# First mixer of a transformer stack: recurrence products cut to 32 keys by 16 queries, inverse products cut to the blocks that the masks keep

## The chip, the cores and the metric

The kernel runs on one core of a Trainium2 chip. The metric is the device time of one execution in microseconds (us), median of several runs. Engines are named as in the profile: PE is TensorE's matmul side, PEld its weight loads, DVE is VectorE, ACT is ScalarE, POOL is GpSimd, SP the queue that issues the weight transfers.

## What is computed

Four layers in a row on 256 tokens of width 2048, all in fp32: a first mixer with two recurrences and an FFN, a second mixer with sparse attention and an FFN, then two small attention layers. The change lies in the first mixer alone. After one large projection it computes, per head (8 of each kind, width 128), over chunks of tokens:

```python
def _hgrn2(q, f_logit, i, lb):            # gated linear recurrence
    ...
    decay = jnp.exp(jnp.where(tril, b[:, :, :, None, :] - b[:, :, None, :, :], -jnp.inf))
    intra = jnp.einsum('bhtd,bhsd,bhtsd->bhts', qn, kn, decay)

def _gated_delta(q, k, v, beta, log_decay):   # delta rule
    ...
    L = jnp.where(tril & ~eye, jnp.einsum('bhncd,bhnsd->bhncs', kb, kc) * decay, 0.0)
    sol = lax.linalg.triangular_solve(L + eye, rhs, left_side=True, lower=True, unit_diagonal=True)
```

## The kernel before, in words

**The main stream.** All large products are `activations x weights`, split in a high and a low part, so that each is three matmuls: 128 tokens stationary, 512 weight columns moving (lines 1124 to 1126 for the projections, 1171 to 1173 for the output matrices). The weights come in slots of 512 KB: SP loads a slot into one of four RAW buffers, ACT writes its high part (line 1669), DVE subtracts to get the low part (line 2197), PE does the slot's 12 matmuls.

**The order.** `write_order` lists by hand every step of the kernel, in one list that each engine walks, doing what it has in each step. Between two slots of the main stream it puts the steps of the mixer: `gdn()` puts the delta rule's, `hgrn(hf)` the gated recurrence's. So on every engine the mixer's work is interleaved with the slots, in a fixed order; an engine that waits in a step holds back all that stands behind it. `gdn()` leaves at least one slot between a product and the next one that needs it.

**The gated recurrence** (`hg_l`, levels l = 0 to 6, for each half hf of the heads: 4 heads, 2 chunks i of 128 tokens). Level l joins blocks of m = 2^l tokens in pairs: the queries of the late block of a pair with the keys of the early one. PE multiplies (line 1391) all 128 keys of a chunk with its 64 late queries, for 4 heads and 2 chunks, 8 products; DVE scales keys and queries for the next level (lines 2522, 2523), multiplies up the spans (`longer`, line 2499) and takes from the product only what the level's mask keeps (`copy_predicated`, line 2534). Level 5 is already cut to 32 keys by 32 queries, two products where the others have one (line 1389), level 6 to 64 keys by 64 queries.

**The delta rule** needs the inverse of a unit lower triangular matrix of 128 x 128 per head, for each (hf, i). Its diagonal blocks of 16 are made on DVE (`gd_w`, `gd_e`). Then for l = 4, 5, 6 two diagonal blocks of m = 2^l are joined: `gd_y` multiplies LT with the inverse so far (line 1271, 4 heads, 128 x 128 each), DVE masks the result into Y (line 2439); `gd_x` multiplies again (line 1289, for l = 6 line 1287) and DVE subtracts the whole product from XX (line 2446); for l = 4 a transpose on DVE follows (line 2449), for l = 6 PE transposes before it (line 1276). Four units (hf, i) make 12 steps of each kind.

Of the kernel before, what the change touches and what calls it, by code (L numbers as in the profile page):

```python
# [10 lines left out]
ALU = mybir.AluOpType  # L11
# [165 lines left out]
def rep(ap, n):  # L177
    return ap.unsqueeze(1).to_broadcast([ap.shape[0], n, ap.shape[1]])


def v3(ap, a):
    return ap.rearrange("p (a b) -> p a b", a=a)
# [601 lines left out]
def build(nc, A, out):  # L784
    with ExitStack() as ctx:
# [9 lines left out]
        def steps(name, line=None, by=1):  # L795
            all_steps.append(Steps(ctx.enter_context(nc.semaphore(name)), line or Line(), by))
            return all_steps[-1]
# [25 lines left out]
        banks = Banks([PS[:, i, :] for i in range(8)])  # L823
# [9 lines left out]
        def w3(o, n, a):  # L833
            return v3(WORK[:, o:o + n], a)
# [24 lines left out]
        MKT, BAND, BLOCK, EYE = WORK[:, 8704:9088], WORK[:, 9088:9216], WORK[:, 9216:9344], WORK[:, 9344:9360]  # L859
# [4 lines left out]
        KBT, QT, LT, QK = (w3(2048 + 512 * j, 512, 4) for j in range(4))  # L864
        XX = WORK[:, 4096:5120].rearrange("p (h x n) -> p h x n", h=4, x=2)
        Y, LTM, S, U = KT, QT, w3(5120, 512, 4), KB
        RV, RW, KD, WT, QE = ADEC, DEC, DEC, KBT, KT

        def gd_cols(hf, i):
# [7 lines left out]
        HX, HK, HQ, HA = (WORK[:, a:a + 1024] for a in (5632, 6656, 7680, 9472))  # L877
# [3 lines left out]
        def of_chunk(x, i):  # L881
            return v3(x, 4)[:, :, 128 * i:128 * i + 128]

        def sides(x, m):
            x = x.rearrange("p (b s m) -> p b s m", s=2, m=m)
            return x[:, :, 0], x[:, :, 1]
# [129 lines left out]
        def slot_of(s):  # L1016
# [3 lines left out]
            if wd < 64:  # L1020
# [10 lines left out]
        v_lo, v_ut, v_ff, v_nm, v_gd, v_cv, v_hg, v_og, v_ns, v_b2, v_rs = (  # L1031
            steps("s_dve_" + n, dve) for n in ("weights", "operand", "ffn", "norm", "gdn", "conv", "hgrn",
                                               "gate", "nsa", "block2", "root"))
# [31 lines left out]
        def tensor(e):  # L1065
# [7 lines left out]
            def take(*name):  # L1073
                b = banks.take(ring, *name)
                on.wait_ge(*banks.free(*name))
                return b
# [189 lines left out]
            @step  # L1266
            def gd_y(hf, i, l):
                b = take("y", hf, i, l)
                on.wait_ge(*(v_gd.of("x", hf, i, l - 1) if l > 4 else v_gd.of("xT", hf, i, 4)))
                for h in range(4):  # L1270
                    x = e.matmul(b[:, 128 * h:128 * h + 128], LT[:, h], XX[:, h, 0], start=True, stop=True)
                x.then_inc(*p_gd.inc("y", hf, i, l))
                if l == 6:
                    b = take("xT", hf, i, l)
                    for h in range(4):
                        x = e.transpose(b[:, 128 * h:128 * h + 128], XX[:, h, 0], ident)
                    x.then_inc(*p_gd.inc("xT", hf, i, l))

            @step
            def gd_x(hf, i, l):  # L1280
                b = take("x", hf, i, l)
                on.wait_ge(*v_gd.of("y", hf, i, l))
                on.wait_ge(*(a_gd if l == 6 else v_gd).of("xT", hf, i, l))
                for h in range(4):
                    o = b[:, 128 * h:128 * h + 128]
                    if l == 6:
                        x = e.matmul(o, Y[:, h], XX[:, h, 1], start=True, stop=True)
                    else:
                        x = e.matmul(o, XX[:, h, 1], Y[:, h], start=True, stop=True)
                x.then_inc(*p_gd.inc("x", hf, i, l))  # L1290

            @step
# [83 lines left out]

            @step
            def hg_l(hf, l):
                rows = 64 if l == 6 else 128
                b = take("hl", hf, l)  # L1380
                on.wait_ge(*v_hg.of("up", hf, l))
                for h in range(4):
                    for i in range(2):
                        late = sides(of_chunk(HQ, i)[:, h], 2 ** l)[1]
                        o = b[0:rows, 128 * h + 64 * i:128 * h + 64 * i + 64].rearrange("p (b m) -> p b m", m=2 ** l)
                        if l == 5:
                            for u in range(2):
                                k = slice(64 * u, 64 * u + 32)
                                x = e.matmul(o[k, u], of_chunk(HK, i)[:, h, k], late[:, u], start=True, stop=True)
                            continue  # L1390
                        x = e.matmul(o, of_chunk(HK, i)[:, h, 0:rows], late, start=True, stop=True)  # L1391
                x.then_inc(*p_hg.inc("s", hf, l))

            @step
# [791 lines left out]
        def vector(e):  # L2186
# [248 lines left out]

            @step
            def gd_y(hf, i, l):
                on.wait_ge(*p_gd.of("y", hf, i, l))
                e.tensor_tensor(Y, v3(banks.ap("y", hf, i, l), 4), rep(MKT[:, 128 * l - 512:128 * l - 384], 4),
                                ALU.mult).then_inc(*banks.empty(v_gd, "y", hf, i, l))  # L2440

            @step
            def gd_x(hf, i, l):
                o = XX[:, :, int(l == 6)]
                on.wait_ge(*p_gd.of("x", hf, i, l))
                e.tensor_tensor(o, o, v3(banks.ap("x", hf, i, l), 4), ALU.subtract).then_inc(*banks.empty(v_gd, "x", hf, i, l))
                if l < 5:
                    on.wait_ge(*v_gd.last())
                    e.transpose(XX[:, :, 1], XX[:, :, 0]).then_inc(*v_gd.inc("xT", hf, i, l + 1))
# [570 lines left out]
```

## Time and profile before

| | |
|---|---|
| median of 3 runs | 2727.71 us (2725.29 to 2728.68) |
| the profiled execution's own time | 2729.03 us |
| its span, first to last instruction | 2727.2 us |
| granted TensorE clock, mean | 0.997 of full |
| busy: PE / PEld / DVE / ACT / POOL | 2694.4 / 2239.4 / 1693.7 / 1343.7 / 63.2 us |
| instructions of PE | 12976 matmuls, 12976 weight loads |
| DMA | 480.55 MB, mean 176 GB/s |

The span is 1.8 us shorter than the execution's own time. The first mixer's projection and recurrences lie in the span's first 460 us. Matmuls are pipelined: the duration of one is longer than the distance from its start to the next one's, so costs on PE are read from starts. In fp32 every product of the mixer shows as two matmul records with a weight load each.

### The profile page before, as it was taken

What the parts mean: (1) busy time and instruction counts of PE and PEld (TensorE: products, weight loads), DVE (VectorE), ACT (ScalarE), POOL (GpSimd) and SP (SyncE); (2) the same over time, 40 slices, a digit from 0 to 9 for tenths busy, and PEclk for the clock granted to TensorE, in tenths of its full rate; (3) what the DMA queues carried; (4) which work ended last, traced back from release to release, by engine and by line L of the source; (5) the groups of instructions that cost most, each with busy time, mean ns of one, the idle gap of its engine ahead of it and who ended that gap; (6) DMA issues with size and microseconds to landing.
All of it is one profiled execution on the core that took longest, in us unless ns stands there. A gap on an engine that the chain in (4) does not pass through costs nothing.

```text
span 2727.2 us, 32273 instructions
## 1 busy us (share of the span) xinstructions
PE 2694.4 (99%) x12976; PEld 2239.4 (82%) x12976; DVE 1693.7 (62%) x2476; ACT 1343.7 (49%) x1952; POOL 63.2 (2%) x85
## 2 busy tenths in 40 slices
PE   9999999999999999999999999999999999999998
PEld 7778888888888888888888888888888888887877
DVE  5677676566666666545555555666666664466666
ACT  6646544464444444434545545544444443355565
POOL 0000000000000000000100000000000000000002
PEclk9999999999999999999999999999999999999999
DMA  7765747666666666556655335566666665565544
GB/s 230 137 139 139 131 125 134 207 190 197 195 193 194 193 195 193 194 194 211 207 166 156 114 109 185 178 193 192 195 194 193 193 196 193 193 202 164 165 137 132
DMA packets 213495, 480.55 MB, mean 176 GB/s; under 512 B 15584, under 2 KB 16480, under 8 KB 212704
## 3 DMA queue, kind: packets, MB, share of 16 engines
q1 hardware_dynamic: 210848, 467.27, 59.0%
q0 software_dynamic: 2352, 11.17, 1.2%
q8 instruction: 102, 1.67, 0.3%
q14 instruction: 49, 0.40, 0.0%
q10 hardware_dynamic: 144, 0.05, 0.0%
HBM read 476.32 MB, written 2.10 MB: 175 GB/s over the span
## 4 chain that ended last, share of the span: by engine, by line
PE 89%; DVE 5%; ACT 3%; DMA 1%; issue 1%; POOL 0%; SPq 0%; ACTq 0%; POOLq 0%
PE PS L1124 19%; PE PS L1126 19%; PE PS L1125 19%; PE PS L1171 8%; PE PS L1172 8%; PE PS L1173 8%; DVE WL L2197 2%; DVE WORK L2364 1%; ACT WH L1669 1%; PE PS L1527 1%; PE PS L1391 1%; PE PS L1099 1%; DVE XL L2197 1%; PE PS L1496 0%; DMA RAW<-in_ffn_w_down 0%
## 5 line engine op out<-in xcount | busy, mean ns | idle before, releaser
L2197 DVE TENSOR_TENSOR WL<-RAW,WH 128x1024 fp32r<-128x1024 f32 x826 | 1010.9, 1225 | 805.2 <-ACT WH L1669 802.9
L1669 ACT ACTIVATE WH<-RAW 128x1024 fp32r<-128x1024 f32 x830 | 875.4, 1056 | 918.0 <-PE PS L1126 606.6
L1124 PE MATMUL PS<-WH,UTH 128*128 128x512 f32 x2396 | 951.9, 397 | 5.9 <-DVE WL L2197 4.9
L1126 PE MATMUL PS<-WH,UTL 128*128 128x512 f32 x2396 | 934.6, 390 | 0.0
L1125 PE MATMUL PS<-WL,UTH 128*128 128x512 f32 x2396 | 934.0, 390 | 0.0
L1124 PEld LDWEIGHTS PS<-WH,UTH 128*128 128x128 f32 x2396 | 450.5, 188 | 102.9 <-DVE WL L2197 5.7
L1126 PEld LDWEIGHTS PS<-WH,UTL 128*128 128x128 f32 x2396 | 450.1, 188 | 96.2
L1125 PEld LDWEIGHTS PS<-WL,UTH 128*128 128x128 f32 x2396 | 450.8, 188 | 88.6
L1171 PE MATMUL PS<-WH,HTH 128*128 128x512 f32 x656 | 255.2, 389 | 0.0
L1173 PE MATMUL PS<-WH,HTL 128*128 128x512 f32 x656 | 255.2, 389 | 0.0
L1172 PE MATMUL PS<-WL,HTH 128*128 128x512 f32 x656 | 255.2, 389 | 0.0
L1171 PEld LDWEIGHTS PS<-WH,HTH 128*128 128x128 f32 x656 | 123.1, 188 | 25.8
L1173 PEld LDWEIGHTS PS<-WH,HTL 128*128 128x128 f32 x656 | 123.1, 188 | 25.6
L1172 PEld LDWEIGHTS PS<-WL,HTH 128*128 128x128 f32 x656 | 123.1, 188 | 25.4
L2292 DVE STREAM_TRANSPOSE WORK<-BIG 32x256 f32<-32x256 f32 x256 | 111.7, 436 | 9.5 <-DVE BIG L2280 0.5
L1171 PE MATMUL PS<-WH,UTH 128*128 128x512 f32 x256 | 102.2, 399 | 1.4 <-DVE UTL L2245 1.4
L1173 PE MATMUL PS<-WH,UTL 128*128 128x512 f32 x256 | 99.9, 390 | 0.0
L1172 PE MATMUL PS<-WL,UTH 128*128 128x512 f32 x256 | 99.8, 390 | 0.0
L2822 POOL TENSOR_TENSOR SM<-SM 128x1 f32<-128x1 f32 (+2 forms) x25 | 28.3, 1134 | 2275.4 <-DVE SM L2201 2275.4
L2197 DVE TENSOR_TENSOR XL<-RAW,XH 128x1024 fp32r<-128x1024 f32 x53 | 63.8, 1219 | 15.1 <-ACT XH L1669 15.0
L1700 ACT ACTIVATE UTH<-PS,GP 128x128 fp32r<-128x128 f32 x160 | 46.2, 387 | 40.3 <-PE PS L1099 40.3
L1669 ACT ACTIVATE XH<-RAW 128x1024 fp32r<-128x1024 f32 x53 | 55.3, 1066 | 21.1 <-DMA RAW<-in_ffn_w_down 8.1
(428 smaller groups left out, 2173.5 us busy)
## 6 DMA issues: line engine op xcount, KB each, us to landing
RAW<-in_ffn_w_gu SPq DMA_DIRECT2D x352, 512.0 KB, 4.4
RAW<-in_ffn_w_down SPq DMA_DIRECT2D x176, 512.0 KB, 4.6
RAW<-in_ab_w_in SPq DMA_DIRECT2D x128, 512.0 KB, 4.8
RAW<-in_nsa_w_in SPq DMA_DIRECT2D x80, 512.0 KB, 3.6
RAW<-in_w_in SPq DMA_DIRECT2D x64, 512.0 KB, 4.1
RAW<-in_ab_w_out SPq DMA_DIRECT2D x32, 512.0 KB, 4.4
RAW<-in_nsa_w_out SPq DMA_DIRECT2D x32, 512.0 KB, 4.1
RAW<-in_w_out SPq DMA_DIRECT2D x16, 512.0 KB, 4.5
```

The costliest lines, as they stand in the source:

```text
L1099: x = e.transpose(b[:, 128 * j:128 * j + 128], H[:, t, 128 * (4 * q + j):128 * (4 * q + j) + 128], ident)
L1124: e.matmul(o, lh, wh[:, j], start=k + j == 0, stop=False)
L1125: e.matmul(o, lh, wl[:, j], start=False, stop=False)
L1126: x = e.matmul(o, ll, wh[:, j], start=False, stop=k + j == NKT - 1)
L1171: e.matmul(o, lh, wh[:, 0, cs], start=k == (0 if hf else LEFT[st][0]), stop=False)
L1172: e.matmul(o, lh, wl[:, 0, cs], start=False, stop=False)
L1173: x = e.matmul(o, ll, wh[:, 0, cs], start=False, stop=k == (KTILES[st] - 1 if hf else LEFT[st][-1]))
L1669: e.activation(wh, raw, ACTF.Copy).then_inc(*a_hi.inc(s))
L1700: e.activation(UTH[:, kk, 128 * t:128 * t + 128], b[:, 128 * j:128 * j + 128], ACTF.Copy, scale=GP[:, st, kk:kk + 1]).then_inc(*a_ut.inc(" ...
L2197: e.tensor_tensor(wl, raw, wh.bitcast(F32), ALU.subtract).then_inc(*v_lo.inc(s))
L2292: e.transpose(out, x).then_inc(*v_ff.inc("hx", st, q, block))
L2822: e.tensor_tensor(o, o, MHALF[:, 0:o.shape[1]], ALU.pow).then_inc(*g_rs.inc("r", *key))
```

## The change

Level 0 to 4 of the gated recurrence: each chunk's product is made as four, of 32 keys and the 16 late queries that lie in the same 32 tokens. Delta rule: each product with the inverse is made only for the blocks that its mask keeps (for l = 4 four blocks of 32 x 16 per head, for l = 5 two of 32 x 32, for l = 6 one of 64 x 64), DVE masks only 64 of 128 columns for l = 6, and subtracts only in these blocks: with four instructions for l = 4, two for l = 5, one for l = 6.

```diff
+        def inverse_blocks(l):
+
+            m = 2 ** l
+            at = range(0, 128, 2 * m)
+            return [(slice(a if l == 4 else a + m, a + 2 * m), slice(a + m, a + 2 * m), slice(a, a + m)) for a in at]
...
         def gd_y, PE:
                 for h in range(4):
-                    x = e.matmul(b[:, 128 * h:128 * h + 128], LT[:, h], XX[:, h, 0], start=True, stop=True)
+                    for rows, late, early in inverse_blocks(l):
+                        x = e.matmul(b[rows, 128 * h + early.start:128 * h + early.stop], LT[:, h, rows], XX[:, h, 0, early],
+                                     start=True, stop=True)
...
         def gd_x, PE:
                 for h in range(4):
-                    o = b[:, 128 * h:128 * h + 128]
-                    if l == 6:
-                        x = e.matmul(o, Y[:, h], XX[:, h, 1], start=True, stop=True)
-                    else:
-                        x = e.matmul(o, XX[:, h, 1], Y[:, h], start=True, stop=True)
+                    for rows, late, early in inverse_blocks(l):
+                        if l == 6:
+                            x = e.matmul(b[early, 128 * h + late.start:128 * h + late.stop], Y[:, h, early], XX[:, h, 1, late],
+                                         start=True, stop=True)
+                        else:
+                            x = e.matmul(b[rows, 128 * h + early.start:128 * h + early.stop], XX[:, h, 1, rows],
+                                         Y[:, h, early], start=True, stop=True)
...
         def hg_l, PE:
+                        keys = of_chunk(HK, i)[:, h]
...
-                        x = e.matmul(o, of_chunk(HK, i)[:, h, 0:rows], late, start=True, stop=True)
+                        else:
+                            for u in range(4):
+                                k, c = slice(32 * u, 32 * u + 32), slice(16 // m * u, 16 // m * (u + 1))
+                                x = e.matmul(o[k, c], keys[:, k], late[:, c], start=True, stop=True)
...
         def gd_y, DVE:
+                n = 64 if l == 6 else 128
-                e.tensor_tensor(Y, v3(banks.ap("y", hf, i, l), 4), rep(MKT[:, 128 * l - 512:128 * l - 384], 4),
+                e.tensor_tensor(Y[:, :, 0:n], v3(banks.ap("y", hf, i, l), 4)[:, :, 0:n],
+                                rep(MKT[:, 128 * l - 512:128 * l - 512 + n], 4),
                                 ALU.mult).then_inc(*banks.empty(v_gd, "y", hf, i, l))
...
         def gd_x, DVE:
-                o = XX[:, :, int(l == 6)]
-                e.tensor_tensor(o, o, v3(banks.ap("x", hf, i, l), 4), ALU.subtract).then_inc(*banks.empty(v_gd, "x", hf, i, l))
+                blocks = inverse_blocks(l)
+                for n, (rows, late, early) in enumerate(blocks):
+                    o, b_n = (XX[early, :, 1, late], b[early, :, late]) if l == 6 else (XX[rows, :, 0, early], b[rows, :, early])
+                    up = banks.empty(v_gd, "x", hf, i, l) if n == len(blocks) - 1 else v_gd.inc("x", hf, i, l, n)
+                    e.tensor_tensor(o, o, b_n, ALU.subtract).then_inc(*up)
```

## Rows read from the trace of the kernel before

**Rows 1.** The page: PE's busy time, and the chain that ended last by engine

```profile
PE 2694.4 (99%) x12976; PEld 2239.4 (82%) x12976; DVE 1693.7 (62%) x2476; ACT 1343.7 (49%) x1952; POOL 63.2 (2%) x85
PE 89%; DVE 5%; ACT 3%; DMA 1%; issue 1%; POOL 0%; SPq 0%; ACTq 0%; POOLq 0%
```

**Rows 2.** Busy time by stretch: stretch, its length, engines with instructions, clock, DMA

```profile
205.00:405.00 200.00, 198.35 (x1202) 171.77 (x1201) 141.57 (x296) 104.62 (x152) 0.00 (x0) 1.00 0.60 132
405.00:425.00 20.00, 18.23 (x100) 14.59 (x99) 16.39 (x47) 10.30 (x13) 2.54 (x1) 1.00 0.47 108
```

**Rows 3.** What PE waited for: us in total, times, longest

```profile
PE PS L1271 <- DVE WORK L2434: 4.8, 2, 3.8
PE PS L1289 <- DVE WORK L2439: 0.2, 1, 0.2
```

**Rows 4.** What DVE waited for, 160 to 460 us

```profile
DVE WORK L2522 <- PE PS L1391: 20.6, 10, 4.3
```

**Rows 5.** PE's timeline: a step of level 4, and a gd_y step; start, us, what

```profile
394.17 1.89 PE L1391 MATMUL PS<-WORK 128*128 128x64 f32 x16
...
396.18 0.40 PE L1125 MATMUL PS<-WL,UTH 128*128 128x512 f32 x1
...
239.79 1.05 PE L1271 MATMUL PS<-WORK 128*128 128x128 f32 x8
...
240.91 0.40 PE L1125 MATMUL PS<-WL,UTH 128*128 128x512 f32 x1
...
247.04 1.05 PE L1271 MATMUL PS<-WORK 128*128 128x128 f32 x8
```

**Rows 6.** Groups by shape, weight loads of the recurrence: 128 and 32 columns

```profile
L1391 PEld LDWEIGHTS PS<-WORK 128*128 128x128 f32 x160 | 19.0, 192 | 0.3
L1389 PEld LDWEIGHTS PS<-WORK 128*32 128x32 f32 x64 | 1.2, 112 | 0.7 <-issue 0.7
```

**Rows 7.** PE's timeline around a step of level 5

```profile
303.16 0.39 PE L1125 MATMUL PS<-WL,UTH 128*128 128x512 f32 x1
303.38 0.39 PE L1126 MATMUL PS<-WH,UTL 128*128 128x512 f32 x1
303.70 0.70 PE L1389 MATMUL PS<-WORK 128*32 128x32 f32 x32
...
304.67 0.39 PE L1125 MATMUL PS<-WL,UTH 128*128 128x512 f32 x1
```

**Rows 8.** Line 1389 alone: matmuls, then weight loads, begun up to 303.80 and 304.20

```profile
303.60:303.80 0.20, 0.10 (x6) 0.10 (x8) 1.00 1.03 195
...
303.60:304.20 0.60, 0.50 (x31) 0.50 (x32) 1.00 1.19 184
```

**Rows 9.** PE's timeline around a step of level 6

```profile
311.73 0.39 PE L1126 MATMUL PS<-WH,UTL 128*128 128x512 f32 x1
312.04 1.15 PE L1391 MATMUL PS<-WORK 128*64 128x64 f32 x16
...
313.45 0.39 PE L1125 MATMUL PS<-WL,UTH 128*128 128x512 f32 x1
```

**Rows 10.** PE's timeline, second mixer: 60 weight columns, two places in turn

```profile
1345.08 3.71 PE L1438 MATMUL PS<-BIG 128*60 128x128 f32 x64
...
1349.06 0.40 PE L1125 MATMUL PS<-WL,UTH 128*128 128x512 f32 x1
```

**Rows 11.** DVE's timeline: the transpose behind gd_x, and three operations in a row

```profile
245.22 0.71 DVE L2449 STREAM_TRANSPOSE WORK<-WORK 128x512 f32<-128x512 f32 x1
...
259.95 0.69 DVE L2523 TENSOR_TENSOR WORK<-WORK 128x512 f32<-128x512 f32 x1
260.55 0.42 DVE L2499 TENSOR_TENSOR BIG<-BIG 128x256 f32<-128x256 f32 x1
260.89 1.30 DVE L2534 COPY_PREDICATED WORK<-MK,PS 128x512 f32<-128x512 uint32 x1
```

More of the change, by code:

```diff
@@ L1378, in hg_l @@
             def hg_l(hf, l):
-                rows = 64 if l == 6 else 128
+                m = 2 ** l
                 b = take("hl", hf, l)
@@ L1383, in hg_l @@
                     for i in range(2):
-                        late = sides(of_chunk(HQ, i)[:, h], 2 ** l)[1]
-                        o = b[0:rows, 128 * h + 64 * i:128 * h + 64 * i + 64].rearrange("p (b m) -> p b m", m=2 ** l)
-                        if l == 5:
+                        keys = of_chunk(HK, i)[:, h]
+                        late = sides(of_chunk(HQ, i)[:, h], m)[1]
+                        o = b[:, 128 * h + 64 * i:128 * h + 64 * i + 64].rearrange("p (b m) -> p b m", m=m)
+                        if l == 6:
+                            x = e.matmul(o[0:64], keys[:, 0:64], late, start=True, stop=True)
+                        elif l == 5:
                             for u in range(2):
                                 k = slice(64 * u, 64 * u + 32)
-                                x = e.matmul(o[k, u], of_chunk(HK, i)[:, h, k], late[:, u], start=True, stop=True)
-                            continue
-                        x = e.matmul(o, of_chunk(HK, i)[:, h, 0:rows], late, start=True, stop=True)
+                                x = e.matmul(o[k, u], keys[:, k], late[:, u], start=True, stop=True)
+                        else:
+                            for u in range(4):
+                                k, c = slice(32 * u, 32 * u + 32), slice(16 // m * u, 16 // m * (u + 1))
+                                x = e.matmul(o[k, c], keys[:, k], late[:, c], start=True, stop=True)
                 x.then_inc(*p_hg.inc("s", hf, l))
@@ L2443, in gd_x @@
             def gd_x(hf, i, l):
-                o = XX[:, :, int(l == 6)]
+                b = v3(banks.ap("x", hf, i, l), 4)
                 on.wait_ge(*p_gd.of("x", hf, i, l))
-                e.tensor_tensor(o, o, v3(banks.ap("x", hf, i, l), 4), ALU.subtract).then_inc(*banks.empty(v_gd, "x", hf, i, l))
+                blocks = inverse_blocks(l)
[3 more added lines that the diff above has]
+                    e.tensor_tensor(o, o, b_n, ALU.subtract).then_inc(*up)
                 if l < 5:
```

## The prediction

> **What bounds the kernel now.** I read the page first. PE is busy for 2694.4 of 2727.2 us, and the chain that ended last runs through PE for 89% [rows 1]. So a microsecond taken from PE's queue is a microsecond of the kernel, unless PE then stands waiting for something with a time of its own. The change lies between 160 and 450 us, so the second view is the busy time of that part by stretch: from 205 to 405 us PE is busy for 198.35 of 200, from 405 to 425 for 18.23 of 20 [rows 2]. The third view is who waits for whom. PE waited for the steps that change in three places only: 4.8 us in two gd_y steps, behind the transpose that ends DVE's own part of the inverse, and 0.2 us in one gd_x step [rows 3]. DVE, the other way, waited 20.6 us for the products of the gated recurrence [rows 4]. DVE is thus ahead of PE almost everywhere, and PE's queue sets the time.
>
> **What a step costs on PE.** Durations mislead here (matmuls overlap), so I read starts. In the main stream one wide matmul follows the other after about 0.23 us (303.16 and 303.38) [rows 7]. A side step is followed by one wide matmul and then another (line 1125); its cost is the distance from its start to that second one, less 0.23. Where there is a gap ahead of the step, I measure from the wide matmul before it, less 0.46.
> - Level 0 to 4: 394.17 to 396.18 us is 2.01, less 0.23: **1.78 us**, rounded up to 1.79 for the small spread of such steps, for 16 instructions of 128 weight columns and 64 moving ones [rows 5], 0.11 each.
> - gd_y, and gd_x likewise: 239.79 to 240.91 us is 1.12, less 0.23: **0.89 us** for 8 instructions [rows 5], again 0.11. The pace is the same for 64 and 128 moving columns, so the weight load sets it. Load durations, 192 ns for 128 columns and 112 for 32, give 80/96 = 0.83 ns a column [rows 6]: 107 ns for 128, 27 ns for 32.
> - Level 5, already cut to 32 x 32, is my model for the new steps. From the wide matmul before it (303.38) to the second after it (304.67) pass 1.29 us; two wide ones would take 0.46: **0.83 us** for 32 instructions [rows 7]. Six had begun at 303.80 and 31 at 304.20 [rows 8]: 25 in 0.40 us, 16 ns each; I take 16.5. The 32 are then 0.53 us, and **0.30 us** is the edge: the way into the narrow form and out of it.
> - Level 6, 64 weight columns in one place: 311.73 to 313.45 is 1.72, less 0.46: **1.26 us** for 16 [rows 9]. Less the edge, 60 ns each.
>
> Why 16.5 and not 27? Level 5 puts its products in turn at two places of the array (output rows 0 to 31 and 64 to 95). The compress step does so with 60 weight columns and 128 moving ones: 3.98 us less 0.23 is 3.75 for 64 instructions, 59 ns each [rows 10], half of the 110 ns that a stream of 128 columns takes in one place [rows 5]. Two places work side by side.
>
> **The change, part by part.**
> 1. Gated recurrence, levels 0 to 4, both halves: 10 steps go from 16 instructions to 64, of 32 weight columns and 16 moving. The nearest row is level 5: same weight load, half the moving columns. 64 x 16.5 = 1.06, plus 0.30: 1.36 us. Saved 1.79 - 1.36 = 0.43 each, **4.3 us**.
> 2. Inverse, l = 4: 8 steps go from 8 instructions to 32 of 32 x 16: 0.53 + 0.30 = 0.83, saved 0.06 each. One of them, at 420 us, ends a stretch that DVE sets; 7 count: **0.4 us**. The first follows PE's longest wait, 3.8 us [rows 3]; I count it like the others.
> 3. l = 5: 8 steps go to 16 instructions of 32 x 32, level 5's form: 0.26 + 0.30 = 0.56, saved 0.33 each: **2.6 us**.
> 4. l = 6: 8 steps keep 8 instructions, now 64 x 64, level 6's form: 0.48 + 0.30 = 0.78, saved 0.11 each: **0.9 us**.
> 5. DVE. Two operations in a row are 0.60 us apart for 512 elements and 0.34 for 256 [rows 11], so about 0.07 plus 1.04 ns an element. Subtracting in four blocks of 64 elements is 0.55 us where it was 0.60, in two of 128 0.41, in one of 256 0.34; masking half the columns for l = 6 saves 0.26. In all about 3 us of DVE's time. I count **nothing**: PE's work on the slots hides it. If small operations cost much more, say 0.27 each, the four take 1.1 us, 0.5 more. Behind them stand the transpose (it ended at 245.93 in one unit) and then gd_y at 247.04 [rows 5, 11]: 1.1 us of cover, enough.
> 6. 736 more matmuls and as many loads (10 x 48, 8 x 24, 8 x 8), 1472 on 25952 of PE, that have to be fetched and issued. The chain shows 1% of "issue" [rows 1], 27 us; 6% of that is 1.5 us at most. I take 0, and keep 1.5 for the range. No wait and no transfer is added; the queues of SP and POOL hold the same work as before.
>
> Sum: 4.3 + 0.4 + 2.6 + 0.9 = **8.2 us**. Against the profiled execution's 2729.03 us this gives 2720.8; that one lies 1.3 us above the median of the runs, so for the median 2727.7 - 8.2 = **2719.5 us**. What is late next: the places where PE waits for DVE (420 us) or for ACT behind the end of a column of weights. They move with PE's queue, because what they wait for itself begins when PE ends a column.
>
> **The pace decides.** Let p be the pace in ns of the steps with four places (parts 1 and 2). The gain is 10 x (1.49 - 0.064p) + 7 x (0.59 - 0.032p) + 3.5 = 22.5 - 0.864p: 8.2 at 16.5, zero at 26. A measurement of this kernel can tell about 0.2%, 5.5 us, from no change: that is p = 19.7. Bounds: from below, four places side by side instead of two, 8 ns, gain 15.6 us; from above, 27 ns, no overlap at all, a loss of 0.8 us.
>
> In this kernel 32 x 32 products begin every 16 ns [rows 8]. The Trainium skill (TensorE: Matmul & The Clock Gate, section "Wait — 56ns, not 53.3ns?") says that matmuls never start closer than about 25 ns apart, however few columns they stream; the row contradicts it. By that rule part 3 would shrink as well, to 8 x (0.89 - 0.70) = 1.5, and the whole gain would be about 0.9 - 1.1 - 1.5 + 1.5, or nothing.
>
> **Rivals.**
> - **A. The full width, four places at once** (2712 us). Level 5 alternates between two places, the new steps among four, with half the moving columns. At 8 ns the gain is 15.6 us. Against it: each product is two instructions in the same place, one after the other, so that at any time only two places may have work, whatever the number of places. The Trainium skill (the same page, Part 3, packing) reports about 2.4 times for three column places. I give a pace clearly under 14 ns a chance of 0.15.
> - **B. An issue floor near 25 ns** (2727.5 us): no change. For it: steps with 64 or 32 instructions of 16 columns could meet a floor that level 5 is too short to show. Against: 16 ns over 25 starts [rows 8]. With a pace between 20 and 26 ns, 0.18.
> - **C. PE runs out of instructions in the long steps** (2730 us), the slower side. Level 5 has 64 instructions counting loads; they can lie ready when the step begins, and no row shows more of them at this pace. The new level steps have 128. If the second half comes only more slowly, here 50 ns a pair, an estimate between 16.5 and the 110 of [rows 5], a step is 0.53 + 1.6 + 0.30 = 2.43 us, 0.64 above now; ten of them lose 6.4 us, and 3.9 us of parts 2 to 4 remain: 2.5 us slower, or 4 us with the 1.5 of part 6. From 30 ns for the second half a level step saves nothing (0.53 + 0.96 + 0.30), and from 42 ns the whole change loses (ten times 0.39 is the 3.9 of the other parts). Chance 0.07.
> - **D. Gains lost to waits**: PE arrives earlier and finds the low part of a weight slot or a scaled key not ready. Against: DVE is busy for 141.57 of 200 us there [rows 2] and waits for PE [rows 4]. It would cost 1 to 4 us, leaving 4 to 7: 0.15.
> - The forecast, pace 14 to 20 ns and nearly all of it kept: 0.45.
>
> **How the numbers follow.** The forecast's own range is 2717 to 2723. Rival A reaches to 2712, D and B to 2727.5. Leaving out C, the far half of B and the far end of A gives 2712.5 to 2726.5. Faster by over 0.2% (under 2722.3): the forecast nearly whole (0.42), A (0.15), a third of D (0.05): 0.62. Within 0.2%: the rest of D and of the forecast, B, half of C: 0.33. Slower: 0.05.
>
> **What would show it.** In the changed kernel's timeline a level step has 64 matmuls of 128x16 and lasts from the wide matmul before it to the second after it 1.82 us, less 0.46 = 1.36 (1.79 now); 64 of them begun in about 1.06 us. gd_y and gd_x cost 0.83, 0.56 and 0.78 us by level. From 205 to 405 us of before, PE's work ends some 6.5 us earlier, and PE's idle time there stays near 1.7 us. I am wrong if the pace is above 20 ns or under 14, if the edge is not 0.30, or if idle time of PE grows by what its steps shrink.

## The result, and the profile after

The changed kernel takes 2712.53 us (median of 4 runs, 2710.66 to 2714.10) where the kernel before takes 2727.43 us: ratio 0.9945, 95% interval 0.9934 to 0.9957, or 14.9 us less. The forecast was 8.2 us less, 2719.5. The sign was right, the gain was 1.8 times the forecast, and the time lies where rival A put it.

The page of the changed kernel, the parts that answer to [rows 1]:

```profile
PE 2679.0 (99%) x13712; PEld 2215.2 (82%) x13712; DVE 1692.9 (62%) x2492; ACT 1343.9 (50%) x1952; POOL 64.0 (2%) x85
PE 89%; DVE 5%; ACT 3%; issue 1%; DMA 1%; POOL 0%; SPq 0%; ACTq 0%; POOLq 0%
```

PE has 736 matmuls more, as counted in part 6, and is busy for 15.4 us less. It is still busy for 99% of the span, and the chain still runs through it for 89%: the bound has not moved.

PE's waits in the first 560 us (us in total, times, longest), to be held against [rows 3]; the last line is for the transposes of a step that does not change:

```profile
PE PS L1279 <- DVE WORK L2450: 4.8, 2, 3.8
PE PS L1299 <- DVE WORK L2456: 0.7, 1, 0.7
PE PS L1374 <- ACT BIG L1742: 1.4, 2, 0.9
```

The kernel before has this instead of the last:

```profile
PE PS L1363 <- ACT BIG L1726: 0.9, 1, 0.9
```

The two waits in `gd_y` are what they were. The one in `gd_x` grew by 0.5 us; it lies in the stretch around 412 us that DVE sets, where the prediction counted no gain for one of two steps. The third line is a new wait of 0.50 us at 331 us: a narrow `gd_x` step ends earlier there, and the transposes behind it in PE's queue then wait for ACT. The pair of them costs 2.02 us in both kernels, so this one step gained nothing. The longer wait stands in the trace of `p_gd_only` too, which cuts the delta rule alone, and not in that of `p_hg_only`, which leaves it whole. All of PE's waits in the 560 us sum to 15.4 us, 14.4 before. Rival D, a gain lost to new waits, thus came in a small way, for the 0.3 us of this step, and not for the 1 to 4 us that it named.

Now the steps themselves, in PE's timeline of the changed kernel (start, duration, what). First a step of the gated recurrence, against [rows 5]:

```profile
280.40 0.39 PE L1133 MATMUL PS<-WH,UTL 128*128 128x512 f32 x1
280.71 0.74 PE L1407 MATMUL PS<-WORK 128*32 128x16 f32 x64
...
281.71 0.39 PE L1132 MATMUL PS<-WL,UTH 128*128 128x512 f32 x1
```

Read as in the prediction: 280.40 to 281.71 is 1.31 us, less 0.46 for two wide matmuls is **0.85 us**. It was 1.79, and 1.36 was forecast. How fast the 64 follow each other shows in the busy time of line 1407 alone; the number after the first x is the matmuls begun:

```profile
280.60:280.80 0.20, 0.09 (x9) 0.09 (x12) 1.00 1.24 256
280.60:281.20 0.60, 0.49 (x57) 0.49 (x60) 1.00 1.15 232
```

48 in 0.40 us are 8.3 ns each, half of the 16.5 assumed. The rest of the step, 0.85 - 64 x 0.0083 = 0.32 us, is the edge, forecast at 0.30.

Then the delta rule, one step for each l (`gd_y` l = 4; `gd_x` l = 5; `gd_x` l = 6), each with the wide matmul before and the second after:

```profile
239.34 0.39 PE L1133 MATMUL PS<-WH,UTL 128*128 128x512 f32 x1
239.65 0.45 PE L1279 MATMUL PS<-WORK 128*32 128x16 f32 x32
...
240.36 0.39 PE L1132 MATMUL PS<-WL,UTH 128*128 128x512 f32 x1
...
251.08 0.39 PE L1133 MATMUL PS<-WH,UTL 128*128 128x512 f32 x1
251.40 0.45 PE L1299 MATMUL PS<-WORK 128*32 128x32 f32 x16
...
252.11 0.39 PE L1132 MATMUL PS<-WL,UTH 128*128 128x512 f32 x1
...
259.24 0.39 PE L1133 MATMUL PS<-WH,UTL 128*128 128x512 f32 x1
259.55 0.68 PE L1296 MATMUL PS<-WORK 128*64 128x64 f32 x8
...
260.50 0.39 PE L1132 MATMUL PS<-WL,UTH 128*128 128x512 f32 x1
```

1.02, 1.03 and 1.26 us, less 0.46 each: **0.56, 0.57 and 0.80 us**, where 0.83, 0.56 and 0.78 were forecast. The steps with two places and with one came out as forecast, within 0.02 us. The steps with four places, and only they, are cheaper. (A place is, as in the prediction, the group of output rows that a product writes.)

The sum with measured steps is 10 x (1.79 - 0.85) = 9.4, 7 x (0.89 - 0.56) = 2.3, 8 x (0.89 - 0.57) = 2.6 and 8 x (0.89 - 0.80) = 0.7: 15.0 us against 14.9 measured.

That the 2.3 comes out is in part luck. Of the eight l = 4 steps, four save 0.32 or 0.33 us, the one at 331 us nothing (above), and the two around 412 us together 0.52. The eighth is the first `gd_y` step, behind PE's wait of 3.8 us. Here is its product in the chain that ended last, before and changed:

```profile
160.93 2.08 PE PS L1271 x8
```

```profile
162.46 0.63 PE PS L1279 x32
```

The granted clock is 0.50 behind this wait in both, from 160.93 to 165.5 us before and from 162.46 to 167.4 in the changed kernel. At this clock the step saves 1.14 us (2.30 to 1.16, from its start to the second wide matmul), but the wide matmuls behind it stay at 0.50 longer in the changed kernel's execution and take 0.58 us more (4.13 instead of 3.55 for the same ten). Net 0.56 us, where the prediction counted this step "like the others". The eight together save 2.4 us.

**A trap in comparing the two traces.** The two profiled executions, 2729.03 and 2712.81 us, are 16.2 us apart, not 14.9. From the first `gd_y` step to the last product of `gd_u` with RW it is 14.9 us: 160.93 to 447.3 before, 162.46 to 433.9 after. The rest lies where neither kernel differs. In the chain of waits of the kernel before, in the second mixer's output matrix (start, duration):

```profile
1695.39 6.59 DMA RAW<-in_nsa_w_out
```

and the same transfer in the changed kernel:

```profile
1681.91 5.32 DMA RAW<-in_nsa_w_out
```

The transfer took 1.3 us more in one execution, PE waited 1.9 us there instead of 0.6, and the stretch of 40 us around it shows a granted clock of 0.96 instead of 1.00. The way from the compress step (1345.1 and 1331.6 us) to the last use of HTH (2435.4 and 2419.0) is 2.9 us longer before: 1.3 of wait, and about 1.6 for 0.04 of clock over 40 us (an estimate from these two numbers). The other way round, the changed kernel's execution loses 1.5 us ahead of the first changed step. Its timeline there:

```profile
135.70 0.50 PE L1131 MATMUL PS<-WH,UTH 128*128 128x512 f32 x1 [2.37 <-DVE WL L2213]
...
137.90 0.63 PE L1132 MATMUL PS<-WL,UTH 128*128 128x512 f32 x1
138.33 0.63 PE L1133 MATMUL PS<-WH,UTL 128*128 128x512 f32 x1
```

After a wait of 2.37 us the wide matmuls come 0.43 us apart instead of 0.23, for some 3 us; the granted clock from 137 to 140 us is 0.50 (1.2 GHz). The kernel before has the same wait, 2.36 us, and its clock stays at 1.00 behind it. Among the other executions profiled below, this dip comes in some and not in others, with the same code there: `e1_32moving` has 0.50, `e3_one_place` 1.00. So spans of single executions are compared by stretch here, and whole kernels by their medians.

### The profile page after: what moved, and what is told of

It reads as the page before. It is cut to its first block, busy times and chain, and to the rows that moved or that the text cites. A ratio compares the mean times of both kernels' runs of the same rounds, so it can differ in the third digit from the quotient of the medians.

```text
span 2711.0 us, 33761 instructions
## 1 busy us (share of the span) xinstructions
PE 2679.0 (99%) x13712; PEld 2215.2 (82%) x13712; DVE 1692.9 (62%) x2492; ACT 1343.9 (50%) x1952; POOL 64.0 (2%) x85
## 4 chain that ended last, share of the span: by engine, by line
PE 89%; DVE 5%; ACT 3%; issue 1%; DMA 1%; POOL 0%; SPq 0%; ACTq 0%; POOLq 0%
PE PS L1131 20%; PE PS L1133 19%; PE PS L1132 19%; PE PS L1178 8%; PE PS L1180 8%; PE PS L1179 8%; DVE WL L2213 2%; DVE WORK L2380 1%; ACT WH L1685 1%; PE PS L1543 1%; PE PS L1106 1%; PE PS L1512 0%; DVE XL L2213 0%; DMA RAW<-in_ffn_w_down 0%; PE PS L1523 0%
## 5 line engine op out<-in xcount | busy, mean ns | idle before, releaser
L2213 DVE TENSOR_TENSOR XL<-RAW,XH 128x1024 fp32r<-128x1024 f32 x53 | 64.0, 1221 | 14.4 <-ACT XH L1685 14.3
```

Source lines behind the costliest of these rows:

```text
L2213: e.tensor_tensor(wl, raw, wh.bitcast(F32), ALU.subtract).then_inc(*v_lo.inc(s))
```

## Experiments

All but `p_hg_only`, which starts from the kernel before, start from the changed kernel, and all ratios are to the kernel before, run beside them. Two theories for the pace of 8.3 ns stood at first. P: the load of 32 weight columns (27 ns) is shared by as many places as are in turn. M: the moving columns set it, 16 against 32 in level 5.

### What sets the pace

**e1_32moving**: twice the moving columns, four places.

```diff
-k, c = slice(32 * u, 32 * u + 32), slice(16 // m * u, 16 // m * (u + 1))
+k, c = slice(32 * u, 32 * u + 32), slice(32 // m * (u // 2), 32 // m * (u // 2 + 1))
```

> Levels 0 to 4 of the gated recurrence: still 32 keys, four places in turn, but each product streams the 32 late queries of its 64 tokens instead of 16; the result is the same. In the changed kernel 64 matmuls begin 8.3 ns apart and a step costs 0.85 us. Theory P (places): the pace is the load of 32 weight columns, 27 ns, shared by four places, plus about 1.6. It expects 8.3 ns again, a step of 0.85 us and the time of the changed kernel, 2712.5 us within 1.5. Theory M (moving columns): with two or more places the pace is set by the moving columns, 0.52 ns each (16.5 for 32, 8.3 for 16). It expects 16.5 ns, a step of 1.38 us, and 10 x 0.53 = 5.3 us more: 2718 us.

Measured: 2711.45 us, ratio 0.9937 (0.9921 to 0.9954), the changed kernel's within the interval. A step in its timeline:

```profile
280.34 0.39 PE L1133 MATMUL PS<-WH,UTL 128*128 128x512 f32 x1
280.65 0.76 PE L1407 MATMUL PS<-WORK 128*32 128x32 f32 x64
...
281.68 0.40 PE L1132 MATMUL PS<-WL,UTH 128*128 128x512 f32 x1
```

1.34 less 0.46 is 0.88 us, a pace of (0.88 - 0.32) / 64 = 8.7 ns. These are products of level 5's own form, 32 x 32, at half of level 5's distance. Theory M falls.

**e2_two_places**: the same products in another order.

```diff
-                for h in range(4):
-                    for i in range(2):
+                for us in (((0, 1), (2, 3)) if l < 5 else (None,)):
+                  for h in range(4):
+                    for i in range(2):
...
-                            for u in range(4):
+                            for u in us:
```

> Levels 0 to 4: the same 32 products of 32 keys by 16 queries, in another order: first all that go to places 0 and 1, then all that go to 2 and 3, so that two places are in turn at any time. Theory P: 27 ns over two places plus some 3, 16.5 ns, a step of 1.38 us, 2718 us. Theory M: 8.3 ns, a step of 0.85 us, 2712.5 us.

Measured: 2714.81 us, ratio 0.9951 (0.9937 to 0.9966). A step:

```profile
280.84 0.39 PE L1133 MATMUL PS<-WH,UTL 128*128 128x512 f32 x1
281.16 1.10 PE L1408 MATMUL PS<-WORK 128*32 128x16 f32 x64
...
282.52 0.39 PE L1132 MATMUL PS<-WL,UTH 128*128 128x512 f32 x1
```

1.22 us, 14.1 ns. Nothing but the order differs from the changed kernel, and the step costs 0.37 us more, 3.7 us over ten. P's direction holds; its 16.5 ns was too much for 16 moving columns. The ratio alone could not tell this from the changed kernel; the timeline does.

**e3_one_place**: `for us in ((0,), (1,), (2,), (3,))`, one place after the other.

> Levels 0 to 4: the same products, place by place: eight products to place 0, then eight to place 1, and so on. Theory P: the weight load alone, 27 ns or more each (30 by the 60 ns of 64 columns in one place), a step of 64 x 30 + 0.32 = 2.24 us, 1.39 more than the changed kernel's: 2726 us. Theory M in its strict form, no cost of the load at all: 16 columns at 0.83 ns, 13 to 15 ns, a step of 1.25 us, 2716.5 us.

Measured: 2724.15 us, ratio 0.9984 (0.9974 to 0.9993). A step:

```profile
280.64 0.39 PE L1133 MATMUL PS<-WH,UTL 128*128 128x512 f32 x1
280.95 1.90 PE L1408 MATMUL PS<-WORK 128*32 128x16 f32 x64
...
283.12 0.39 PE L1132 MATMUL PS<-WL,UTH 128*128 128x512 f32 x1
```

2.02 us, 26.6 ns a matmul. Between 281.40 and 282.40 us 40 matmuls begin, 25 ns each, so the pace read directly is near. The step is more than the 1.79 us of the full product of the kernel before: in this order the cut of levels 0 to 4 is a loss, and only the delta rule's part of the gain is left.

**e4_8moving**: 64 products of 32 keys by 8 queries.

```diff
-                            for u in range(4):
-                                k, c = slice(32 * u, 32 * u + 32), slice(16 // m * u, 16 // m * (u + 1))
+                            for u in range(8):
+                                k = slice(32 * (u // 2), 32 * (u // 2) + 32)
...
+                                x = e.matmul(o[k, at[0], at[1]], keys[:, k], late[:, at[0], at[1]], start=True, stop=True)
```

> Levels 0 to 4: each product cut again, 32 keys by 8 queries, 64 products (128 matmuls with 128 loads) a step, two in a row to the same place, four places. The result is the same. Theory P: the load binds, 8.3 ns each, 128 x 8.3 = 1.06, a step of 1.38 us: 2718 us. Theory M: 4.2 ns, a step of 0.85 us, no change. Rival C of the prediction (instructions run short in long steps): the pace of the later ones is above that of the first, and the step costs more than 1.5 us, above 2719 us.

Measured: 2720.91 us, ratio 0.9970 (0.9960 to 0.9981). A step:

```profile
280.41 0.39 PE L1133 MATMUL PS<-WH,UTL 128*128 128x512 f32 x1
280.73 1.40 PE L1411 MATMUL PS<-WORK 128*32 128x8 f32 x128
...
282.39 0.39 PE L1132 MATMUL PS<-WL,UTH 128*128 128x512 f32 x1
```

1.52 us, (1.52 - 0.32) / 128 = 9.4 ns. Fewer moving columns bring nothing here, though the kernel also differs in having four matmuls in a row to the same place, and the two were not separated. The step is just above the 1.5 us, and the time above the 2719 us, that were named for rival C. But rival C's sign was a pace that gets worse within the step, and it does not: 44 matmuls begin from 281.10 to 281.50 us and 43 from 281.50 to 281.90. Rival C, which needed 42 ns for the second half of a step of 128 instructions, is out; the changed kernel's own step of 128 instructions at 8.3 ns says the same.

Three more kernels, run once each, then asked what the 27 and the 8 ns are. **e5_one_place_16keys** (e3's order) and **e7_four_places_16keys** (the changed kernel's) change `32 * u + 32` to `32 * u + 16` in the slice of the keys; they leave half of the keys' products out, so they serve for the timing alone. **e6_one_place_32moving** has e1's slice in e3's order.

> Levels 0 to 4 place by place, as in e3_one_place (26.6 ns a matmul there), but each product takes only the first 16 of its 32 keys, so it loads 16 weight columns and leaves the other keys' half of the product out. If the load binds at one place, the pace falls to about half, 13 to 15 ns, and a step costs 1.2 us. If the 26.6 ns are a fixed distance between two matmuls in the same place, it stays at 26 to 27, 2.0 us.

> Levels 0 to 4 place by place, 32 keys, each product with 32 late queries instead of 16; the result is the same. If the load binds, 27 to 30 ns and a step of about 2.1 us. If loading and streaming in one place follow each other, 16 more columns cost 13 ns more: 40 ns, a step of 2.9 us.

> Levels 0 to 4 with four places in turn as in the change (8.3 ns), but each product takes only 16 of its 32 keys and leaves the rest out. If the load shared by four places still binds, 4 to 5 ns and a step of 0.6 us. If 8.3 ns is a floor of another kind (a distance below which no matmul with its load is issued), it stays, and the step costs 0.85 us.

2720.55, 2723.41 and 2710.79 us, too few runs to rest on; what counts is their steps, in this order:

```profile
281.67 0.39 PE L1133 MATMUL PS<-WH,UTL 128*128 128x512 f32 x1
281.98 1.53 PE L1408 MATMUL PS<-WORK 128*16 128x16 f32 x64
...
283.78 0.39 PE L1132 MATMUL PS<-WL,UTH 128*128 128x512 f32 x1
```

```profile
282.05 0.39 PE L1133 MATMUL PS<-WH,UTL 128*128 128x512 f32 x1
282.37 1.91 PE L1408 MATMUL PS<-WORK 128*32 128x32 f32 x64
...
284.54 0.39 PE L1132 MATMUL PS<-WL,UTH 128*128 128x512 f32 x1
```

```profile
278.61 0.39 PE L1133 MATMUL PS<-WH,UTL 128*128 128x512 f32 x1
278.93 0.70 PE L1407 MATMUL PS<-WORK 128*16 128x16 f32 x64
...
279.89 0.39 PE L1132 MATMUL PS<-WL,UTH 128*128 128x512 f32 x1
```

1.65, 2.03 and 0.82 us. All paces together, with 0.32 us taken off each step as the edge:

| kernel | places in turn | keys x queries | step, us | pace, ns |
|---|---|---|---|---|
| e3 | 1 | 32 x 16 | 2.02 | 26.6 |
| e6 | 1 | 32 x 32 | 2.03 | 26.7 |
| e5 | 1 | 16 x 16 | 1.65 | 20.8 |
| level 5, before | 2 | 32 x 32 | 0.83 | 16 |
| e2 | 2 | 32 x 16 | 1.22 | 14.1 |
| changed kernel | 4 | 32 x 16 | 0.85 | 8.3 |
| e1 | 4 | 32 x 32 | 0.88 | 8.7 |
| e7 | 4 | 16 x 16 | 0.82 | 7.8 |
| e4 | 4 | 32 x 8 | 1.52 | 9.4 |

The number of places is the strong term: 26.6, 14.1, 8.3 ns for one, two and four. Moving columns up to 32 hardly count: 26.6 and 26.7 ns in one place, 8.3 and 8.7 in four. (With two places the rows are 14.1 and 16 ns, but from two different steps.) The number of keys counts at one place, but not in proportion: half the load takes away 5.8 of 26.6 ns, so e5 agrees with neither of its two expectations, and load time is part of the distance in one place, not all of it. At four places half the load takes away 0.5 ns of 8.3: theory P's 27 / 4 is not the explanation there. Something near 8 ns a matmul with its load stands below, and what it is stays open.

### Which part of the change brings what

**p_hg_only** has the cut of levels 0 to 4, with `gd_y` and `gd_x` as before on both engines; **p_gd_only** the reverse.

> Only the gated recurrence's levels 0 to 4 are cut to 32 keys by 16 queries; the delta rule is that of the kernel before, on PE and on DVE. Theory 1 (PE's steps add up): ten steps cost 0.85 instead of 1.79 us, 9.4 us less than the kernel before, ratio 0.9966. Theory 2 (the prediction's pace of 16.5 ns, two places active): 4.3 us less, ratio 0.9984.

> Only the delta rule's products and their subtraction are cut; levels 0 to 4 of the gated recurrence are those of the kernel before. Theory 1: l = 4 0.33 us each, of which seven count, 2.3; l = 5 eight times 0.32, 2.6; l = 6 eight times 0.09, 0.7: 5.6 us less, ratio 0.9979. Theory 2: 3.9 us less, 0.9986. If a wait takes part of it, less than 3 us.

Measured: 2718.37 us, ratio 0.9964 (0.9951 to 0.9976), and 2721.99 us, ratio 0.9980 (0.9971 to 0.9989). Of 2727.33 us that is 9.8 and 5.5 us, with 9.4 and 5.6 expected from the steps (the medians alone differ by 9.0 and 5.3). Together 15.3, so the parts add up to the whole's 14.9 within their intervals of about 3 us to either side. The 4.3 us that the prediction had for the recurrence would be a ratio of 0.9984, outside the first interval.

**p_hg_dve** adds to p_hg_only the change's DVE part alone, PE keeping the full products:

```diff
-                    for rows, late, early in inverse_blocks(l):
-                        x = e.matmul(b[rows, 128 * h + early.start:128 * h + early.stop], LT[:, h, rows], XX[:, h, 0, early],
-                                     start=True, stop=True)
+                    x = e.matmul(b[:, 128 * h:128 * h + 128], LT[:, h], XX[:, h, 0], start=True, stop=True)
```

> The gated recurrence cut as in the change; the delta rule with the change's DVE part (four, two or one subtraction of the kept blocks, half the columns masked for l = 6), but with PE's full products of the kernel before; the result is the same. Against p_hg_only it is DVE's part of the change alone. The prediction counts it at nothing: the same time within 1 us. Rival: DVE's smaller work shortens the two stretches that it sets (at 160 and 412 us), up to 1.5 us less; or the four small subtractions, 0.95 us in the trace against 0.69 before, delay the next product, up to 1.5 us more.

Measured: 2717.51 us, ratio 0.9962 (0.9948 to 0.9975), 0.9 us under p_hg_only. That is in line with no effect, but the intervals, some 3.5 us to either side, are too wide to rule out the 1.5 us of the rivals. The traces say why little was to be expected: PE's waits for `gd_y` and `gd_x` are the same in both (4.8 and 0.2 us). In the changed kernel four subtractions together are busy for 0.95 us, and DVE's transpose begins 0.99 us after their first, against 0.72 before. PE never waits for that transpose, so the cover was enough. In the kernel before (the transpose behind it is in [rows 11]):

```profile
244.50 0.69 DVE L2446 TENSOR_TENSOR WORK<-WORK,PS 128x512 f32<-128x512 f32 x1 [0.20 <-PE PS L1289]
```

In the changed kernel:

```profile
244.00 0.95 DVE L2468 TENSOR_TENSOR WORK<-WORK,PS 32x64 f32<-32x64 f32 x4
244.99 0.71 DVE L2471 STREAM_TRANSPOSE WORK<-WORK 128x512 f32<-128x512 f32 x1
```

### A version that goes further

**v2_diagonal**: in the changed kernel `hg_g` multiplies all 128 keys by all 128 queries and keeps, by the identity mask, the diagonal. Here it makes four products of 32 by 32 along the diagonal instead, one for each place.

```diff
-                        x = e.matmul(b[:, 128 * h:128 * h + 128], of_chunk(HK, i)[:, h], of_chunk(HQ, i)[:, h],
-                                     start=True, stop=True)
+                        for u in range(4):
+                            k = slice(32 * u, 32 * u + 32)
+                            x = e.matmul(b[k, 128 * h + 32 * u:128 * h + 32 * u + 32], of_chunk(HK, i)[:, h, k],
+                                         of_chunk(HQ, i)[:, h, k], start=True, stop=True)
```

> The changed kernel, and besides it the recurrence's diagonal product, of which the identity mask keeps only the diagonal, as four products of 32 keys by 32 queries instead of one of 128 by 128 (two such steps in the kernel, 16 matmuls each before, 64 after). The full step costs 1.79 us. Theory P (four places, 8.3 ns also with 32 moving columns, as in e1_32moving): 64 x 8.3 + 0.32 = 0.88 us, 0.9 less in each half, 1.8 us less than the changed kernel, 2710.7 us. If the products of the two chunks do not follow each other closely, the edge is paid twice, 1.2 us less. No gain if DVE's masking behind the product sets the time there.

Measured: 2709.46 us, ratio 0.9934 (0.9921 to 0.9946). In the changed kernel a narrow `gd_y` step and the full product behind it run from 245.98 to 248.79 us:

```profile
245.98 0.39 PE L1133 MATMUL PS<-WH,UTL 128*128 128x512 f32 x1
246.29 0.45 PE L1279 MATMUL PS<-WORK 128*32 128x32 f32 x16
246.67 2.05 PE L1384 MATMUL PS<-WORK 128*128 128x128 f32 x16
...
248.79 0.39 PE L1132 MATMUL PS<-WL,UTH 128*128 128x512 f32 x1
```

In v2_diagonal the same two steps:

```profile
242.99 0.39 PE L1133 MATMUL PS<-WH,UTL 128*128 128x512 f32 x1
243.31 0.35 PE L1279 MATMUL PS<-WORK 128*32 128x32 f32 x10
...
243.57 0.74 PE L1386 MATMUL PS<-WORK 128*32 128x32 f32 x60
...
244.58 0.39 PE L1132 MATMUL PS<-WL,UTH 128*128 128x512 f32 x1
```

2.81 us against 1.59: 1.22 us less, more than the 0.9 expected, and the trace shows the matmuls of the two narrow steps interleaved; that they pay one edge between them fits this, but is read from one place alone. In the other half the step stands behind transposes of full width (from the `gd_y` step's start to the second wide matmul 3.13 us in the changed kernel, 2.22 in this one), and the saving is 0.91. That is 2.1 us in all. The two intervals overlap, so the kernels' times alone do not separate them; the steps do.

## Why the prediction was wrong in size

- **The step that failed** is the term that parts 1 and 2 share: "The nearest row is level 5: same weight load, half the moving columns. 64 x 16.5 = 1.06". It measured 0.53 us. Level 5 is nearest in the shape of one product, but not in the number of places in turn, and e2 and e3, which change only the order, show that the places set the pace. Part 1 was sized 4.3 us and brought 9.4, part 2 0.4 and brought 2.3; these two make 7.0 us more, 15.0 by the steps.
- **The reason given against rival A fell**: "each product is two instructions in the same place, one after the other, so that at any time only two places may have work". e2 and e3 keep these pairs and change only how many places follow each other; with four the pace is 8.3 ns, with two 14.1. The pairs do not hold the other places back. Rival A named half the moving columns beside the four places; of the two only the places count (e1).
- Part of the sign was on record: level 5's 16 ns with two places against 27 ns for one load [rows 6, 8]. An argument that no row showed was weighed above its continuation to four places. The other row given for places side by side does not show it: [rows 10] has 60 weight columns at 59 ns in two places, held against 128 columns, but [rows 9] has 64 columns at 60 ns in one place, so there the second place brought nothing visible. 59 ns is about what 128 moving columns take in the main stream (0.23 us for 512, a quarter of it, an estimate). The 8 ns taken as the bound from below is almost exact: the formula 22.5 - 0.864p gives 15.3 us at 8.3 ns.
- **Right**: the bound (PE's queue) and that PE's savings arrive nearly whole; the edge (0.30 forecast, 0.32 measured); parts 3 and 4 (0.56 and 0.78 us forecast, 0.57 and 0.80 measured); DVE's part at nothing, as far as p_hg_dve can tell; the extra instructions at nothing (the steps' sum leaves no remainder).
- **Off without effect**: part 5 priced the four small subtractions at 0.55 us; they take 0.99, more than the 0.72 of the one before, and DVE's busy time fell by 0.8 us and not by about 3. The prediction's own allowance of 1.1 us for them covers it.
- **Rival B**, a floor near 25 ns, is refuted at 8.3 ns. The rule of the Trainium skill that stood beside it (TensorE: Matmul & The Clock Gate, section "Wait — 56ns, not 53.3ns?"), that starts are never closer than about 25 ns, does not hold here with two or four places; in one place 32 keys come near it (26.6 ns) and 16 keys go below it (20.8). The packing that the Trainium skill measured (same page, section "Part 3: Packing small matmuls — row/col tiling", about 2.4 times for three column places) points the right way: here four places make 26.6 / 8.3 = 3.2 times.
- **Rival C** is refuted by e4 and by the changed kernel's own step. **Rival D** came for one step, 0.3 us.

## What to carry to other kernels

Cutting a full product into four blocks of 32 keys pays here only if the small products go to different output rows in turn; the same 32 products in another order cost 0.85, 1.22 or 2.02 us, and the last is more than the full product's 1.79. Price a narrow step as its number of matmuls times the pace for its places, plus an edge of about 0.3 us between full-width work, and put narrow steps next to each other, where they seem to share it (v2_diagonal). When a term is taken from the nearest row, ask which property of that row sets its time before calling it near.

## What was not expected of the hardware

- With four places in turn fp32 matmuls, each with its weight load, follow each other every 8.3 ns with 16 moving columns, 8.7 with 32, and still 7.8 with half the keys.
- In one place the distance is 26.6 ns for 32 keys and still 20.8 for 16: it does not follow the load in proportion.
- Overlap between output places does not need different rows of the array: all products here use all 128 rows. The Trainium skill (TensorE: Matmul & The Clock Gate, section "Part 3: Packing small matmuls — row/col tiling") says in its list of what overlaps that weight loads overlap with running matmuls only where the row groups differ. e3 against the changed kernel, 26.6 against 8.3 ns, shows that work of different places overlaps without that: a load of 32 columns alone was worked out at 27 ns [rows 6], so loads that follow every 8.3 ns run beside something. Whether beside matmuls or beside other loads, these distances do not tell.
